# Delta-rule stage: calls of TensorE, ScalarE and VectorE in another order, the first heads' solve steps between the levels of the second half's inverse

## The chip, the core and the metric

The kernel runs on one core of a Trainium2 chip. The metric is device time in microseconds for one launch, and less is better. A core has TensorE (PE, matrix products, with its weight loads shown apart as PEld), VectorE (DVE), ScalarE (ACT, functions looked up in a table set that is loaded beforehand), GpSimd (POOL) and DMA queues, here all issued by SyncE (SP). The engines run side by side, each through its own list of instructions in the order in which the program was written, and they wait for each other on semaphores.

## The reference, cut to what matters

Two blocks of two layers each for 256 tokens of width 1024 in fp32. The change touches only the gated delta rule of the second block:

```python
def gdn_mixer(h, w_in, conv_w, a_log, dt_bias, o_norm, w_out):
    proj = h @ w_in
    qkv, z, a, b = jnp.split(proj, [3 * W, 4 * W, 4 * W + H], axis=-1)
    qkv = jax.nn.silu(causal_depthwise_conv(qkv, conv_w))
    q, k, v = jnp.split(qkv, 3, axis=-1)
    q, k = l2_norm(q), l2_norm(k)               # per head of 128
    beta = jax.nn.sigmoid(b)
    g = -jnp.exp(a_log) * jax.nn.softplus(a + dt_bias)
    o = chunk_gated_delta_rule(q, k, v, g, beta)
    o = rms_norm_2(o, o_norm) * jax.nn.silu(z)
    return o @ w_out
...
def chunk_gated_delta_rule(q, k, v, g, beta):
    gcum = jnp.cumsum(gc, axis=-1)
    decay = jnp.where(causal, jnp.exp(gcum[..., :, None] - gcum[..., None, :]), 0.0)
    a_mat = jnp.where(strict, jnp.einsum('bhncd,bhnsd->bhncs', kb, kc) * decay, 0.0)
    sol = lax.linalg.triangular_solve(a_mat, rhs, left_side=True, lower=True, unit_diagonal=True)
    u, w = sol[..., :Dv], sol[..., Dv:]
    attn = jnp.einsum('bhncd,bhnsd->bhncs', qc, kc) * decay
    ...
```

There are 8 heads of 128. Before and after this stage, the change leaves every call where it was.

## The kernel before, in words

**Weights.** All weights are cut into 136 chunks of at most 128 x 2048. A chunk is loaded by DMA into one of three `raw` buffers, ACT copies it to a rounded half (`hi(c)`, `whi<-raw`), DVE subtracts to get the rest (`lo(c)`, `wlo<-raw,whi`), and PE multiplies both halves in four quarters, `quarter(c, 0..3)`. On PE a call `to(c, q)` issues every quarter up to `(c, q)`. The delta-rule stage has chunks 94 to 114: 94 to 106 make k, q and v, 107 to 110 make z, 111 to 114 are the output product. A chunk's `hi` waits until PE has done all four quarters of the chunk three before it.

**The delta rule in 128-token tiles.** For head h, `conv_pre(i)` (DVE), `conv_acc(i)` (ACT) and `conv_taps(i)` (DVE, six instructions) are the convolution of two of the 24 column groups, `conv_silu` and `v_silu` its silu. `qk_square(h)` (ACT), `sums(h)` (PE) and `sum_add(h)` (DVE) are the norms; `ln_sums` (ACT) takes the logarithm of all of them. `row_bc(h)` (PE, `ps<-spread,pick`) spreads a row of log decays over the partitions, `decay_arg(h)` (DVE) adds the column part, `decay(h)` (ACT, two instructions) exponentiates, `kq(h)` (PE, `ps<-arena`) makes the products of keys with keys and queries, and `block_(h)` (DVE) multiplies them by the decays.

**The inverse and the solve.** Heads go in groups g of two (0 to 3; heads 0 to 3 are the first half, 4 to 7 the second). The triangular inverse of a group starts from 8x8 blocks (`inv_c`, `inv_d`, `inv_r`, `inv_b`, `inv_e`, `inv_0`) and doubles them in the levels 3 to 6: `inv_w`, `inv_x` and `inv_v` on PE, with a copy out of PSUM on ACT (`inv_w`, `inv_y`) and an addition on DVE (`inv_x`) between them; `inv_f`, `inv_t`, `inv_y` finish it. The solve of head h has four steps on PE, `sol(h, 0)` to `sol(h, 3)`, with ACT copying out of PSUM after the steps 0, 2 and 3 and DVE after step 1. Then the output norm: `out_squares`, `rsq("gdn_o0")` (ACT: a logarithm, then an exponential), `rsq_b`, `out_norm`, `out_T`, `out_hi`, `out_lo`.

**What sets the order.** It is written out by hand, one list of calls for each engine (PE from L1223, ACT from L2190, DVE from L3500, POOL from L3815), and an engine never runs a call ahead of one that stands before it. Small products of PE share four PSUM banks, 4 to 7, taken in turn (`ring`, L505): a call that takes a bank first waits until the engine that reads the call four banks back has read it. So `row_bc` and `kq` also wait for the decays (semaphore `g_ed`, one count for each `decay(h)`) and for the blocks (`g_ba`) of earlier heads, and `sol(3, 3)` waits for ACT's copy of `sol(3, 2)` (`g_sa3`).

**Tables.** `table(name)` (L1469) asks for a table set by an explicit load. Where an activation's function isn't in the set that is loaded at that place of ACT's list, the build puts a load of its own ahead of that activation; it then bears the line of the activation (L1467 before, L1469 after) and not that of `table`. In the kernel before, every function finds its set loaded by `table`.

Of the kernel before, what the change touches and what calls it, by code (L numbers as in the profile page):

```python
# [131 lines left out]
def bass_two_blocks(nc, A, out):  # L132

    ctx = ExitStack()
    with ctx:
# [358 lines left out]
        def tensor_program(eng):  # L494
# [745 lines left out]
            to(104, 2)  # L1240
            sums(6)
            sums(7)
            to(105, 0)
            rw_T()
            kq(0)
            row_bc(0)
            row_bc(1)
            to(106, 0)
# [12 lines left out]
            kq(5)  # L1261
            inv_c(0)
            row_bc(6)
            to(108, 0)
            inv_r(0)
            row_bc(7)
            to(108, 1)
            kq(6)
            to(109, 0)
            inv_0(1)  # L1270
            inv_0(0)
            kq(7)
            to(109, 1)
            inv_w(1, 3)
            inv_w(0, 3)
            to(109, 2)
            inv_x(0, 3)
            inv_x(1, 3)
            to(109, 3)
            inv_v(0, 3)  # L1280
            inv_v(1, 3)
            inv_w(0, 4)
            inv_w(1, 4)
            v_T(0, 0)
            v_T(0, 1)
            inv_x(0, 4)
            inv_x(1, 4)
            to(110, 0)
            v_T(1, 0)
            inv_v(1, 4)  # L1290
            inv_w(1, 5)
            v_T(1, 1)
            inv_v(0, 4)
            inv_w(0, 5)
            inv_x(1, 5)
            to(110, 1)
            inv_x(0, 5)
# [15 lines left out]
            sol(0, 0)  # L1313
            sol(1, 0)
            to(111, 0)
            inv_y(1)
# [13 lines left out]
            sol(2, 1)  # L1330
            inv_x(2, 3)
            inv_v(3, 3)
            inv_w(3, 4)
            inv_v(2, 3)
            sol(3, 1)
# [128 lines left out]
        def scalar_program(eng):  # L1464
# [4 lines left out]
            def table(name):  # L1469
                eng.preload_act_table_set(name)  # L1470
# [755 lines left out]
            qk_square(1)
            conv_silu(4)
            hi(105)
            conv_silu(5)
            conv_acc(7)  # L2230
            qk_square(2)
            qk_square(3)
            conv_silu(6)
            qk_square(4)
            qk_square(5)
            conv_silu(7)
# [15 lines left out]
            decay(5)  # L2252
            decay(6)
            hi(110)
# [1908 lines left out]
```

How the kernel before makes its waits and increments, by code:

```python
    def wait_ge(self, sem, v):  # L58
        if self.seen.get(sem.num, 0) < v:
            self.seen[sem.num] = v
            self.e.wait_ge(sem, v)
# [6 lines left out]
    def settle(self, n=None):  # L68
        self.wait_ge(self.own, self.n if n is None else n)
# [429 lines left out]
            def take(b, sem_, v):  # L499
                if hold[b] is not None:
                    L.wait_ge(*hold[b])
                hold[b] = (sem_, v)
# [20 lines left out]
            def x_ready(stage, j2):  # L524
                L.wait_ge(s_xlo, 4 * XROUND[stage] + j2 + 1)
# [1 line left out]
            def x_ready_kv(j2, t):  # L527
                L.wait_ge(s_flo, 4 * t + j2 + 1)
# [1 line left out]
            def quarter(c, q):  # L530
                d = CHUNKS[c]
                kind, stage = d["kind"], d["st"]
                wh, wl = wk(whi, c), wk(wlo, c)
                if c < 2 and q == 0:
                    if c == 1:
                        L.wait_ge(s_l0, 4)
                elif c == SPLIT:
                    if q == 0:
                        L.wait_ge(s_l0, 8)
                    elif q == 1:
                        L.wait_ge(*LO[c])
                elif 2 <= c < 5 and q % 2 == 0:
                    L.wait_ge(*((s_l0, c + 3) if q == 0 else LO[c]))
                elif q == (1 if kind == "uq" else 0):
                    if stage[:3] == "mlp" and kind == "pw" and (c not in UP or d["hk"] == 0):
                        L.wait_ge(s_hi, c + 1)
                    else:
                        L.wait_ge(*LO[c])
                tok = None
# [3343 lines left out]
            def finish():  # L3893
                eng.wait_ge(s_out, 80)
```

## Time and profile before

| | |
|---|---|
| median of 3 runs | 893.73 us (893.17 to 894.28) |
| the profiled execution, its own time | 893.27 us |
| its span | 891.1 us |
| PE / PEld busy | 881.4 / 767.6 us (99 / 86%) |
| DVE / ACT / POOL busy | 632.1 / 521.7 / 38.6 us (71 / 59 / 4%) |
| mean granted clock of TensorE | 1.000 |
| HBM | 141.85 MB read, 160 GB/s over the span |
| table loads on ACT | 8, of 1283 ns each, 3 of them in the delta-rule stage |

A busy share is the time in which an engine has an instruction running. Matmuls are pipelined: each shows a duration longer than the distance to the next one, so starts are compared with starts. The span lies from the first to the last instruction; the rest of the 893.27 us lies around it. Times in rows are microseconds from the start of the span. Where the same kind of instruction stands several times in a row, the trace's order merges them into one line with a count.

### The profile page before, as it was taken

What the parts mean: (1) busy time and instruction counts of PE and PEld (TensorE: products, weight loads), DVE (VectorE), ACT (ScalarE), POOL (GpSimd) and SP (SyncE); (2) the same over time, 40 slices, a digit from 0 to 9 for tenths busy, and PEclk for the clock granted to TensorE, in tenths of its full rate; (3) what the DMA queues carried; (4) which work ended last, traced back from release to release, by engine and by line L of the source; (5) the groups of instructions that cost most, each with busy time, mean ns of one, the idle gap of its engine ahead of it and who ended that gap; (6) DMA issues with size and microseconds to landing.
All of it is one profiled execution on the core that took longest, in us unless ns stands there. A gap on an engine that the chain in (4) does not pass through costs nothing.

```text
span 891.1 us, 13047 instructions
## 1 busy us (share of the span) xinstructions
PE 881.4 (99%) x5231; PEld 767.6 (86%) x5231; DVE 632.1 (71%) x1067; ACT 521.7 (59%) x851; POOL 38.6 (4%) x48
## 2 busy tenths in 40 slices
PE   9999999999999999999999999999999999999997
PEld 8878888888888888888888888999989987798885
DVE  7986877766575667567656556679899867767774
ACT  6997443454445677645444435466556756747782
POOL 0151000000000000000000000000014310000000
PEclk9999999999999999999999999999999999999999
DMA  8722455454745454347455654555241312654511
GB/s 313 242 95 100 185 167 211 163 193 166 248 149 188 143 189 158 126 150 242 176 194 183 223 197 150 157 177 182 65 180 49 121 46 66 219 213 142 189 48 47
DMA packets 60876, 143.72 MB, mean 161 GB/s; under 512 B 4497, under 2 KB 6673, under 8 KB 60817
## 3 DMA queue, kind: packets, MB, share of 16 engines
q1 hardware_dynamic: 60816, 142.91, 46.3%
q8 instruction: 41, 0.67, 0.3%
q14 instruction: 19, 0.15, 0.0%
HBM read 141.85 MB, written 1.05 MB: 160 GB/s over the span
## 4 chain that ended last, share of the span: by engine, by line
PE 95%; DVE 2%; ACT 2%; DMA 1%; issue 0%; SPq 0%; DVEq 0%
PE ps L513 90%; PE ps L521 5%; ACT arena L1467 1%; DMA raw<-mla_w_in_dram 1%; ACT whi L1467 0%; DVE arena_r L2456 0%; DVE sub L2456 0%; DVE arena L2766 0%; DVE wlo L2456 0%; ACT xhl L1467 0%; DVE X L2462 0%; DVE st L2462 0%; ACT L1470 0%; DVE arena L2456 0%; DVE xhl L2462 0%
## 5 line engine op out<-in xcount | busy, mean ns | idle before, releaser
L2456 DVE TENSOR_TENSOR wlo<-raw,whi 128x2048 fp32r<-128x2048 f32 (+4 forms) x141 | 300.0, 2137 | 104.8 <-ACT whi L1467 104.7
L1467 ACT ACTIVATE whi<-raw 128x2048 fp32r<-128x2048 f32 (+6 forms) x143 | 251.6, 1771 | 158.5 <-PE ps L513 144.0
L513 PE MATMUL ps<-xhl,whi 128*128 128x512 f32 (+1 forms) x912 | 199.6, 346 | 0.0
L513 PEld LDWEIGHTS ps<-xhl,whi 128*128 128x128 f32 x912 | 155.1, 188 | 19.9 <-DVE xhl L2462 0.2
L513 PE MATMUL ps<-whi,xhl 128*128 128x512 f32 (+2 forms) x528 | 167.2, 385 | 0.4 <-DVE xhl L2462 0.3
L513 PE MATMUL ps<-whi,oth 128*128 128x512 f32 x416 | 165.4, 398 | 0.0
L513 PE MATMUL ps<-whi,otl 128*128 128x512 f32 x416 | 162.3, 390 | 0.0
L513 PE MATMUL ps<-wlo,oth 128*128 128x512 f32 x416 | 162.1, 390 | 0.0
L513 PE MATMUL ps<-xhl,wlo 128*128 128x256 f32 x704 | 121.6, 283 | 0.0
L513 PEld LDWEIGHTS ps<-whi,xhl 128*128 128x128 f32 x528 | 98.3, 189 | 18.4 <-issue 1.8
L513 PEld LDWEIGHTS ps<-xhl,wlo 128*128 128x128 f32 x704 | 103.0, 191 | 3.2 <-DVE wlo L2456 0.2
L513 PE MATMUL ps<-wlo,xhl 128*128 128x512 f32 (+2 forms) x264 | 99.3, 378 | 0.3 <-DVE wlo L2456 0.3
L513 PEld LDWEIGHTS ps<-whi,otl 128*128 128x128 f32 x416 | 78.1, 188 | 16.7
L513 PEld LDWEIGHTS ps<-whi,oth 128*128 128x128 f32 x416 | 78.2, 188 | 15.5 <-issue 0.3
L513 PEld LDWEIGHTS ps<-wlo,oth 128*128 128x128 f32 x416 | 78.2, 188 | 15.0
L1467 ACT ACTIVATE arena<-ps 128x256 f32<-128x256 f32 (+4 forms) x138 | 52.2, 417 | 66.3 <-PE ps L513 61.2
L2456 DVE TENSOR_TENSOR arena<-ps,arena 128x256 f32<-128x256 f32 (+3 forms) x106 | 46.7, 469 | 40.6 <-ACT arena L1467 28.2
L513 PE MATMUL ps<-arena 128*128 128x128 f32 (+3 forms) x384 | 64.0, 318 | 0.5 <-ACT arena L1467 0.5
L513 PEld LDWEIGHTS ps<-arena 128*128 128x128 f32 (+1 forms) x384 | 54.6, 190 | 7.0 <-issue 1.6
L1467 ACT ACTIVATE arena<-ps,st 128x512 f32<-128x512 f32 (+2 forms) x64 | 39.4, 643 | 33.1 <-PE ps L513 15.1
L513 PEld LDWEIGHTS ps<-wlo,xhl 128*128 128x128 f32 x264 | 49.6, 188 | 7.7 <-DVE wlo L2456 0.6
L1467 ACT ACTIVATE arena<-arena 128x512 f32<-128x512 f32 (+4 forms) x68 | 39.4, 606 | 4.1 <-DVE arena L2462 2.2
(150 smaller groups left out, 827.3 us busy)
## 6 DMA issues: line engine op xcount, KB each, us to landing
raw<-mlp_w_in_dram SPq DMA_DIRECT2D x32, 1024.0 KB, 5.3
raw<-mlp_w_out_dram SPq DMA_DIRECT2D x32, 1024.0 KB, 4.9
raw<-gdn_w_in_dram SPq DMA_DIRECT2D x16, 1024.0 KB, 5.3
raw<-moba_w_qkv_dram SPq DMA_DIRECT2D x12, 1024.0 KB, 5.1
raw<-kv_w_dram SPq DMA_DIRECT2D x8, 1024.0 KB, 5.4
raw<-fox_w_in_dram SPq DMA_DIRECT2D x8, 1024.0 KB, 5.1
raw<-mla_w_o_dram SPq DMA_DIRECT2D x4, 1024.0 KB, 4.8
raw<-moba_w_o_dram SPq DMA_DIRECT2D x4, 1024.0 KB, 6.2
```

Source lines behind the costliest of these rows:

```text
L513: return eng.matmul(o, l, r, start=start, stop=True, skip_group_check=True)
L521: return eng.transpose(o, i, ident)
L1467: return eng.activation(o, i, f, **kw)
L2456: return eng.tensor_tensor(o, a, b, f)
```

## The change

Nothing is added to or taken from the program as it is written, except that `table("natural_log_exp_and_others")` ahead of `ln_sums()` is gone, that `table("silu_and_others")` and `table("natural_log_exp_and_others")` now stand together behind `decay(1)`, where one `table("silu_and_others")` stood behind `decay(7)`, and that calls stand in another order. On PE the small products and the quarters of weights they stand between are in another order from chunk 101 to chunk 112. `decay(h)` calls on ACT now have `conv_acc`, `v_silu(0)` and `hi` between them in another pattern. The diff, cut to the places that matter:

```diff
 # PE
+            kq(1)
+            row_bc(2)
+            to(105, 3)
+            row_bc(3)
             to(106, 1)
-            row_bc(3)
             kq(2)
-            to(106, 3)
+            to(106, 2)
+            kq(3)
             row_bc(4)
+            row_bc(5)
+            to(107, 0)
+            kq(4)
+            row_bc(6)
             to(107, 1)
-            kq(3)
-            kq(4)
-            row_bc(5)
+            kq(5)
+            row_bc(7)
+            to(107, 2)
+            inv_c(0)
             to(107, 3)
-            kq(5)
-            inv_c(0)
-            row_bc(6)
...
             inv_0(3)
+            sol(2, 0)
             inv_0(2)
             sol(0, 2)
-            sol(2, 0)
+            sol(1, 2)
             inv_w(3, 3)
+            sol(3, 0)
             inv_w(2, 3)
-            sol(3, 0)
-            sol(1, 2)
...
-            sol(2, 2)
+            inv_x(3, 4)
             sol(3, 2)
-            inv_x(3, 4)
+            sol(2, 1)
             inv_x(2, 4)
             sol(3, 3)
+            sol(2, 2)
             inv_v(3, 4)
             inv_v(2, 4)
+            inv_w(2, 5)
+            out_T(0)
+            inv_w(3, 5)
+            inv_x(2, 5)
             sol(2, 3)
 # ACT
             qk_square(7)
-            table("natural_log_exp_and_others")
             ln_sums()
-            conv_acc(8)
-            conv_acc(9)
+            hi(107)
             decay(0)
             decay(1)
-            hi(107)
+            table("silu_and_others")
+            table("natural_log_exp_and_others")
+            conv_acc(8)
             decay(2)
+            decay(3)
+            conv_acc(9)
+            conv_acc(10)
             hi(108)
-            decay(3)
             decay(4)
-            hi(109)
+            v_silu(0)
             decay(5)
             decay(6)
-            hi(110)
             decay(7)
-            table("silu_and_others")
-            conv_acc(10)
+            hi(109)
+            z_silu(0, 0)
+            inv_0(1)
             conv_acc(11)
-            v_silu(0)
-            inv_0(1)
...
             inv_w(2, 4)
-            sol(2, 2)
+            rsq("gdn_o0")
             sol(3, 2)
             table("natural_log_exp_and_others")
-            rsq("gdn_o0")
             sol(3, 3)
+            sol(2, 2)
 # DVE
             decay_arg(0)
             decay_arg(1)
-            conv_taps(8)
+            conv_pre(9)
             block_(0)
             lo(107)
             block_(1)
-            conv_taps(9)
-            inv_0(0)
             decay_arg(2)
             decay_arg(3)
+            conv_taps(8)
+            conv_taps(9)
             block_(2)
+            conv_pre(10)
+            inv_0(0)
             decay_arg(4)
-            conv_pre(10)
+            block_(3)
+            decay_arg(5)
```

**ACT, the decays of heads 4 to 6, before.** `arena<-ps5,st 128x256` and its like are the first instruction of a `decay`, `arena<-arena 128x2x256` the second; `whi1<-raw1` is `hi(109)`, `whi2<-raw2` is `hi(110)`.

```order
L1467 ACTIVATE arena<-ps5,st 128x256 [waits g_dt]
L1467 ACTIVATE arena<-arena 128x2x256
L1467 ACTIVATE whi1<-raw1 128x2048 [waits s_w,s_raw1]
L1467 ACTIVATE arena<-ps6,st 128x256 [waits g_dt]
L1467 ACTIVATE arena<-arena 128x2x256
L1467 ACTIVATE arena<-ps6,st 128x256 [waits g_dt]
L1467 ACTIVATE arena<-arena 128x2x256
L1467 ACTIVATE whi2<-raw2 128x2048 [waits s_w,s_raw2]
L1467 ACTIVATE arena<-ps4,st 128x256 [waits g_dt]
L1467 ACTIVATE arena<-arena 128x2x256
```

And now; `arena<-arena 128x1024` is `v_silu(0)`, `arena<-arena,small` is `conv_acc(10)`:

```order
L1469 ACTIVATE arena<-arena,small 128x256 [waits g_pre]
L1469 ACTIVATE arena<-arena,small 128x256
L1469 ACTIVATE whi0<-raw0 128x2048 [waits s_w,s_raw0]
L1469 ACTIVATE arena<-ps7,st 128x256 [waits g_dt]
L1469 ACTIVATE arena<-arena 128x2x256
L1469 ACT_TABLE_LOAD
L1469 ACTIVATE arena<-arena 128x1024 [waits g_cv]
L1469 ACT_TABLE_LOAD
L1469 ACTIVATE arena<-ps4,st 128x256 [waits g_dt]
L1469 ACTIVATE arena<-arena 128x2x256
```

`v_silu(0)` stands between `decay(4)` and `decay(5)`, with a load that the build placed on each side of it, and `conv_acc(10)` and `hi(108)` stand ahead of `decay(4)`; `hi(109)` moved behind `decay(7)`.

**PE, the keys' products of head 5, before.** `ps0` and `ps1` with `whi2,xhl` are quarters of chunk 107, `arena 128x2x128` opens `kq(5)` (four instructions), `own8,otl` is `inv_c(0)`, `spread,pick` is `row_bc(6)`.

```order
L513 MATMUL ps1<-whi2,xhl 128x512 [waits g_pre]
L513 MATMUL ps1<-wlo2,xhl 128x512
L513 MATMUL ps1<-whi2,xhl 128x512 x2
L513 MATMUL ps1<-wlo2,xhl 128x512
L513 MATMUL ps1<-whi2,xhl 128x512
L513 MATMUL ps7<-arena 128x2x128 [waits g_ba]
L513 MATMUL ps4<-arena 128x128
L513 MATMUL ps7<-arena 128x2x128
L513 MATMUL ps4<-arena 128x128
L513 MATMUL ps5<-own8,otl 128x8 [waits g_id1,g_id0]
L513 MATMUL ps5<-own8,otl 128x8 x7
L513 MATMUL ps6<-spread,pick 128x2x128 [waits g_ed]
```

And now, where the first `spread,pick` is `row_bc(6)`, then comes one quarter of chunk 107, `kq(5)`, and `row_bc(7)`:

```order
L513 MATMUL ps7<-spread,pick 128x2x128 [waits g_ed]
L513 MATMUL ps7<-spread,pick 128x2x128
L513 MATMUL ps0<-whi2,xhl 128x512 [waits g_pre,s_lod]
L513 MATMUL ps0<-wlo2,xhl 128x512
L513 MATMUL ps0<-whi2,xhl 128x512 x2
L513 MATMUL ps0<-wlo2,xhl 128x512
L513 MATMUL ps0<-whi2,xhl 128x512
L513 MATMUL ps4<-arena 128x2x128 [waits g_ba,g_ed]
L513 MATMUL ps5<-arena 128x128
L513 MATMUL ps4<-arena 128x2x128
L513 MATMUL ps5<-arena 128x128
L513 MATMUL ps6<-spread,pick 128x2x128 x2
```

Two quarters of chunk 107 that stood ahead of `kq(5)` now stand behind it, `row_bc(6)` now stands ahead of it, and it now waits for `g_ed`, which for this bank is the count of `decay(5)`, beside `g_ba`.

**ACT, the first output norm, before.** The first row is the copy of `inv_w(2, 4)`, the two `st<-st` are `rsq("gdn_o0")`, `arena<-ps` with `g_sp2`, `g_sp3` the copies of `sol(2, ..)` and `sol(3, ..)`, those of 128x256 of their last steps.

```order
L1467 ACTIVATE arena_r<-ps6 128x512 [waits g_ip2]
L1467 ACTIVATE arena<-ps7 128x128 [waits g_sp2]
L1467 ACTIVATE arena<-ps4 128x128 [waits g_sp3]
L1470 ACT_TABLE_LOAD
L1467 ACTIVATE st<-st 128x4 [waits s_rm]
L1467 ACTIVATE st<-st 128x4 [waits o_act]
L1467 ACTIVATE arena<-ps7 128x256 [waits g_sp3]
L1467 ACTIVATE arena_r<-ps4 128x512 [waits g_ip3]
```

And now, from the copies of `inv_y(2, 3)` and `inv_w(2, 4)` on:

```order
L1469 ACTIVATE arena_r<-ps4 128x512 [waits g_ip2]
L1469 ACTIVATE arena_r<-ps5 128x512 [waits g_ip2]
L1469 ACT_TABLE_LOAD
L1469 ACTIVATE st<-st 128x4 [waits s_rm]
L1469 ACT_TABLE_LOAD
L1469 ACTIVATE st<-st 128x4 [waits o_act]
L1469 ACTIVATE arena<-ps7 128x128 [waits g_sp3]
L1472 ACT_TABLE_LOAD
L1469 ACTIVATE arena<-ps6 128x256 [waits g_sp3]
L1469 ACTIVATE arena<-ps7 128x128 [waits g_sp2]
```

`rsq("gdn_o0")` stands ahead of the copy of `sol(3, 2)`, with a load ahead of each of its two instructions, and the load of `table` follows behind that copy.


Beside these, the build places loads of its own ahead of `ln_sums()`, `decay(0)` and `z_silu(0, 0)`. With them and those of the rows above ACT's list has 15 loads in place of 8: 10 from `ln_sums()` to `rsq("gdn_o0")` in place of 3.

## Rows read from the trace of the kernel before

**Rows 1.** The page: chain that ended last, shares of the span by engine
```profile
PE 95%; DVE 2%; ACT 2%; DMA 1%; issue 0%; SPq 0%; DVEq 0%
```

**Rows 2.** Windows: span, busy us (count) of PE, PEld, DVE, ACT, POOL; clock; DMA
```profile
630.00:697.00 67.00, 67.00 (x464) 61.83 (x463) 61.14 (x123) 36.93 (x56) 14.08 (x10) 1.00 0.26 94
697.00:718.00 21.00, 20.26 (x161) 18.78 (x160) 15.94 (x41) 17.55 (x39) 7.32 (x7) 1.00 0.48 176
```

**Rows 3.** Waits of PE: who waited for whom, us in total, times, longest us
```profile
PE ps L521 <- DVE arena_r L2456: 0.6, 2, 0.3
...
PE ps L521 <- DVE X L2462: 0.3, 1, 0.3
```

**Rows 4.** Timeline of ACT: start us, us, instruction, xcount, [idle before <-releaser]
```profile
629.54 1.28 ACT L1470 ACT_TABLE_LOAD   x1
...
665.65 0.63 ACT L1467 ACTIVATE arena<-arena 128x512 f32<-128x512 f32 x1
666.30 1.28 ACT L1470 ACT_TABLE_LOAD   x1
667.59 1.71 ACT L1467 ACTIVATE arena<-arena,small 128x256 f32<-128x256 f32 x4
```

**Rows 5.** Timeline of PE around the end of quarter (104, 3)
```profile
634.54 0.38 PE L521 MATMUL ps<-small,st 128*32 128x128 f32 x2
```

**Rows 6.** Timeline of ACT: the two instructions of decay(4), then hi(109)
```profile
652.19 0.48 ACT L1467 ACTIVATE arena<-ps,st 128x256 f32<-128x256 f32 x1
652.55 0.64 ACT L1467 ACTIVATE arena<-arena 128x512 f32<-128x512 f32 x1
653.07 1.92 ACT L1467 ACTIVATE whi<-raw 128x2048 fp32r<-128x2048 f32 x1
```

**Rows 7.** Groups of ACT, 597 to 730 us, shapes apart: v_silu
```profile
L1467 ACT ACTIVATE arena<-arena 128x1024 f32<-128x1024 f32 x2 | 2.1, 1063 | 0.0
```

**Rows 8.** Timeline of DVE: decay_arg(0) and (1), conv_taps(8), block_(0), lo(107)
```profile
636.51 1.66 DVE L2462 SCALAR_TENSOR_TENSOR arena<-ps,st,cap 128x256 f32<-128x256 f32 x4 [0.54 <-PE ps L513]
638.09 2.45 DVE L2462 SCALAR_TENSOR_TENSOR arena<-arena,small 128x255 f32<-128x255 f32 x6
640.45 1.02 DVE L2462 SCALAR_TENSOR_TENSOR arena<-ps,arena 128x512 f32<-128x512 f32 x2
641.38 2.28 DVE L2456 TENSOR_TENSOR wlo<-raw,whi 128x2048 fp32r<-128x2048 f32 x1
```

**Rows 9.** Timeline of PE: kq(1), row_bc(4), last product of quarter (107, 2), kq(5)
```profile
642.30 1.47 PE L513 MATMUL ps<-arena 128*128 128x256 f32 x8
...
649.70 0.47 PE L513 MATMUL ps<-spread,pick 128*128 128x256 f32 x2
...
658.40 0.39 PE L513 MATMUL ps<-whi,xhl 128*128 128x512 f32 x1
658.63 1.47 PE L513 MATMUL ps<-arena 128*128 128x256 f32 x8
```

**Rows 10.** Timeline of ACT: from the copy of inv_y(3, 3) to rsq("gdn_o0")
```profile
707.07 2.20 ACT L1467 ACTIVATE arena_r<-ps 128x512 fp32r<-128x512 f32 x4
709.17 0.44 ACT L1467 ACTIVATE arena<-ps 128x128 f32<-128x128 f32 x2
709.63 1.28 ACT L1470 ACT_TABLE_LOAD   x1
710.92 0.45 ACT L1467 ACTIVATE st<-st 128x4 f32<-128x4 f32 x2
```

**Rows 11.** Timeline of PE: inv_0(3) and (2), sol(3, 3), inv_v(2, 5)
```profile
701.00 1.32 PE L521 MATMUL ps<-small,arena_r 128*128 128x128 f32 x8 [0.29 <-DVE arena_r L2456]
...
709.94 0.88 PE L513 MATMUL ps<-arena 128*128 128x128 f32 x6
...
715.03 0.66 PE L521 MATMUL ps<-small,arena_r 128*128 128x128 f32 x4 [0.32 <-DVE arena_r L2456]
```

**Rows 12.** Timeline of PE: the first matmuls of the program
```profile
1.18 4.85 PE L513 MATMUL ps<-spread 128*128 128x256 f32 x21 [1.18 <-DVE spread L2758]
```

More of the change, by code:

```diff
@@ L1312, in tensor_program @@
             to(110, 3)
-            sol(0, 0)
             sol(1, 0)
             to(111, 0)
+            sol(0, 0)
             inv_y(1)
@@ L2263, in scalar_program @@
             inv_w(1, 3)
-            inv_y(0, 3)
+            hi(110)
             inv_y(1, 3)
-            inv_w(0, 4)
             inv_w(1, 4)
             v_silu(1)
+            inv_y(0, 3)
+            inv_w(0, 4)
             hi(111)
@@ L2276, in scalar_program @@
             inv_w(1, 6)
+            z_silu(0, 1)
             inv_y(0, 5)
@@ L2279, in scalar_program @@
             inv_t(0)
-            z_silu(0, 0)
-            z_silu(0, 1)
+            z_silu(1, 0)
+            sol(1, 0)
             inv_t(1)
-            z_silu(1, 0)
             sol(0, 0)
-            sol(1, 0)
             hi(113)
             inv_0(3)
+            sol(2, 0)
             inv_0(2)
             sol(0, 2)
-            sol(2, 0)
+            sol(1, 2)
+            sol(3, 0)
             inv_w(3, 3)
             inv_w(2, 3)
-            sol(3, 0)
-            sol(1, 2)
             z_silu(1, 1)
@@ L3545, in vector_program @@
             rT_copy()
-            conv_pre(9)
+            conv_pre(8)
             decay_arg(0)
             decay_arg(1)
-            conv_taps(8)
+            conv_pre(9)
             block_(0)
@@ L3552, in vector_program @@
             block_(1)
-            conv_taps(9)
-            inv_0(0)
             decay_arg(2)
             decay_arg(3)
+            conv_taps(8)
+            conv_taps(9)
             block_(2)
+            conv_pre(10)
+            inv_0(0)
             decay_arg(4)
-            conv_pre(10)
-            lo(108)
-            block_(3)
-            block_(4)
-            inv_0(1)
-            decay_arg(5)
-            lo(109)
+            block_(3)
+            decay_arg(5)
+            inv_0(1)
+            conv_pre(11)
+            block_(4)
+            decay_arg(6)
+            lo(108)
             block_(5)
             inv_d(0)
-            decay_arg(6)
             decay_arg(7)
+            inv_0(2)
             inv_b(0)
-            conv_pre(11)
             inv_e(1)
@@ L3577, in vector_program @@
             block_(7)
-            inv_0(3)
+            inv_x(1, 3)
             inv_x(0, 3)
-            inv_x(1, 3)
+            v_beta(0, 0)
             lo(110)
-            v_beta(0, 0)
+            inv_x(1, 4)
             v_beta(0, 1)
-            inv_0(2)
-            inv_x(1, 4)
             inv_x(0, 4)
             v_beta(1, 0)
+            inv_0(3)
             lo(111)
-            v_beta(1, 1)
             inv_x(1, 5)
             inv_x(0, 5)
+            v_beta(1, 1)
             lo(112)
@@ L3601, in vector_program @@
             inv_b(1)
-            inv_e(2)
             inv_e(3)
@@ L3605, in vector_program @@
             sol(1)
+            inv_e(2)
             sol(0)
@@ L3608, in vector_program @@
             inv_x(3, 3)
+            inv_x(2, 3)
+            out_sums(0)
+            sol(3)
+            inv_x(3, 4)
             sol(2)
-            inv_x(2, 3)
-            sol(3)
-            out_sums(0)
-            inv_x(3, 4)
+            rsq_b("gdn_o0")
             inv_x(2, 4)
-            rsq_b("gdn_o0")
             out_norm(0)
+            out_lo(0)
             inv_x(2, 5)
-            out_lo(0)
             inv_x(3, 5)
@@ L3625, in vector_program @@
             inv_s(2)
+            inv_f(2)
             inv_s(3)
-            inv_f(2)
             inv_f(3)
             inv_y(2)
+            out_lo(1)
             inv_y(3)
-            out_lo(1)
+            sol(4)
             sol(5)
-            sol(4)
             sol(7)
```

137 lines of the change are left out of this document (65 added, 72 removed).

## The prediction, made before the changed kernel ran

> **What bounds the kernel now.** I read the chain first: PE holds 95% of it [rows 1]. Then the windows of the delta-rule stage: PE is busy for all of 630 to 697 and for 20.26 of the next 21 us [rows 2]. Then PE's waits: in the whole stage the views show three over 0.25 us, two for DVE's inverse and one of 0.3 for the residual behind the output product [rows 3, 11]. So PE has hardly anything to gain: its instructions are the same before and after, and what an order can bring is the sum of these waits and some tenths that pass when PE changes from one kind of product to another, about 1.8 us. What an order can cost has no such bound, since each small product waits on DVE or ACT, and ACT is busy for 17.55 of the 21 us of the second half [rows 2]. So I looked last at the timeline of ACT and at what its list now holds.
>
> **What is added on ACT.** The written calls are the same but for one `table`, yet the list now has 10 table loads from `ln_sums()` to `rsq("gdn_o0")` in place of 3, since `table` no longer stands where the function's kind changes and the build fills in. A load shows 1.28 us; the one at 666.30 begins 0.02 us after the second instruction of a decay ends (665.65 + 0.63) and the next activation starts 0.01 us behind it [rows 4]. So I price a load at 1.28 us of ACT, and seven more at 9.0 us. ACT is busy for 36.93 of 67 us in the first part, so most of it could lie in idle time; what counts is which loads stand ahead of something that PE waits for.
>
> The page "ScalarE: Activation LUTs" of the Trainium skill (What ACT_TABLE_LOAD costs) gives the same 1283 ns and adds a drain of some 1380 ns for every switch to another set, 2.66 us in all. The rows show no such gap on either side of a load [rows 4], so the sum goes without it; with it, it would be the rival named below.
>
> **First half, in the time base of before.** Four steps.
>
> 1. `hi(107)` now stands ahead of `decay(0)`. It needs all quarters of chunk 104, whose last ends at 634.7 (the next product starts at 634.54 and the tail of the pipeline is 0.16) [rows 5]. It takes 1.9 [rows 6], so it ends at 636.6. The build's load follows to 637.9, `decay(0)` to 638.9 and `decay(1)` to 639.8 (0.99 for one, 0.90 more for the next) [rows 6]. PE is at `kq(1)` 2.9 us earlier than at 642.30, since two quarters of 12 products at 0.12 moved behind it: 639.4 [rows 9]. By the banks it needs `decay(1)`. Wait: 0.45.
> 2. The two loads of `table` stand behind `decay(1)`: ACT is at `conv_acc(8)` at 642.4 and done at 643.3. DVE does `block_(0)` from 638.95, `lo(107)`, `block_(1)` and two `decay_arg`, 0.93 + 2.2 + 0.93 + 1.6, to 644.6, so that the two loads are hidden. Then it does `conv_taps(8)` and `(9)`, 2.37 each, to 649.35 and `block_(2)` to 650.4 [rows 8]. PE's `row_bc(4)` needs that block's bank. It comes to it at 649.70 + 1.23 for `kq(3)`, now ahead, less 1.44 for a quarter, now behind, plus the 0.45 of step 1: 649.95 [rows 9]. Wait: 0.45.
> 3. `conv_acc(10)` on ACT waits for `conv_pre(10)`, 0.6 us behind `block_(2)` on DVE; it runs from 651.0 to 651.85, `hi(108)` to 653.65, `decay(4)` to 654.6 [rows 6]. Then a load, `v_silu(0)` with 1.06 [rows 7], a load: 658.25. `decay(5)` ends at 659.25.
> 4. PE's `kq(5)` needs `decay(5)` by its bank. It stood at 658.63; two quarters of six products at 0.23 moved behind it and `row_bc(6)` with 0.32 ahead of it: 656.2, and with the waits so far 657.1 [rows 9]. It starts at 659.3. Wait: 2.2.
>
> Together 3.1. A wait of PE is not made good later in this stage, since PE has no idle time there [rows 2]. Behind `kq(5)` stand the quarters of chunks 107 and 108 and all of the first inverse; DVE's `block_(5)` and `inv_d(0)` wait for PE in turn, and so ACT's `decay(7)`, `hi(109)` and DVE's `lo(109)` come late by about the same, not by more: I find `lo(109)` done at 672.9 and PE at quarter (109, 0) at 675.7. The load ahead of `z_silu(0, 0)` falls where ACT waits for PE anyway, and costs nothing; if it weren't covered it would cost 1.28. That the order of the first half itself saves nothing I take from the calls issued up to quarter (110, 1), which are the same. I book 3.2, for the first matmul behind a wait starts with its weights not yet loaded (some 0.05 each). The bounds: without any cost of the build's loads, `decay(0)` to `decay(5)` come 1.3 to 3.9 us earlier and no step waits, so 0; with every load that stands ahead of `decay(5)` on the path (1 + 2 + 2) and nothing hidden, 6.4.
>
> **Second half, in the time base of before.** PE's `inv_0(2)` now waits for DVE's `inv_e(2)`, which moved behind `inv_y(1)` and `sol(1)`: about 0.5, in place of the 0.29 at 701.00 [rows 11]. That is even. Then `rsq("gdn_o0")` moved ahead of the copy of `sol(3, 2)`. Of the four copies at 707.07 the last ends at 709.27 [rows 10]; the order brings it to 709.1. A load to 710.4, the logarithm 0.24, a load to 711.9, the exponential 0.2, and the copy of `sol(3, 2)` 0.28: 712.4 [rows 10]. PE's `sol(3, 3)` needs that copy; it stood at 709.94 [rows 11], and comes to 709.7 with `sol(2, 2)` behind it. It starts at 712.45, 2.5 us later than before. Behind it stand ten small products and their copies. The load of `table` puts ACT at the copies of `sol(3, 3)` and of `inv_y(3, 4)` at 713.7, so `inv_x(2, 5)`, `inv_x(3, 5)` and `inv_v(2, 5)` wait 0.3, 0.3 and 0.15 by my count, in place of the 0.32 and 0.25 that PE waits there before (at 715.03 and behind it) [rows 11]. Even again. So 2.5. Bounds: 0, if the two loads lay in idle time, and 3.9, if the third load is paid too.
>
> **What is moved and costs nothing.** On PE 1.3 to 1.8 us of waits could go in the second half; the two entries above keep them. Behind chunk 111 the solve of the last four heads has the same distance from copy to use (four steps of 0.22). `hi(114)` and `lo(114)` moved ahead of `out_hi(2)` and `out_lo(2)`; these end at 737.8 where PE comes to quarter (113, 0) at about 737.9, so this is covered only just, and would cost a tenth or two. The wait of 0.3 for the residual [rows 3] is there before and after, since it hangs on the last product of the stage. The DMA queue's list is the same, and a load of weights starts when DVE is done with the chunk three before it; DMA is busy for 0.26 of the time [rows 2].
>
> **Sum.** 893.27 for the profiled execution, of which 891.1 is the span, and 3.2 + 2.5: 899.0. The execution lies 0.46 under the median of the runs shown, 893.73, so by the median it would be 899.4; I say 899.1. A difference under 0.2% (1.8 us) I count as no change.
>
> **Rivals.**
>
> - *The loads are free.* If ACT loads a set that it has at hand in no time, or if all seven fall into idle time, the order's own saving stays: in the second half PE comes to inv_v(3, 5) 1.8 us earlier, less 0.5 for `inv_0(2)`. That gives 892.0, faster. For it speaks that ACT is idle for 30 of the 67 us [rows 2]; against it that the load in rows 4 takes its full time with work right behind it, and that it decides only if `decay(5)` is done by 657.1, two loads earlier than counted. 5%.
> - *Part is hidden.* One of the two waits of 2 us is shorter, because DVE's blocks come earlier than I count or because ACT reaches a load early: 896.0 to 897.5. The first wait hangs on a chain of fifteen durations. 12%, and 3% more that both are mostly hidden: 893 to 895.
> - *More waits behind the long ones.* The copies of the second half are tight on every engine (waits under 0.1 us everywhere by my reading), and each load that I hid could show: one more load, 1.28, and a few tenths: 900.5 to 902.5. 12%.
> - *The clock falls.* All rows show a granted clock of 1.00 (2.4 GHz). PE idles 2.2 and 2.7 us at once, where before it never idled over 0.5 in this stage. The first 21 products of the program, behind an idle engine, stand 0.23 apart [rows 12], the same shape later 0.12. If PE ran at 1.2 GHz for two quarters behind each wait, that would add 2 x 2.8: 904.6. Nothing in the rows shows a fall inside the program. 5%.
> - *A drain with each load.* 1.38 more for each of the three loads on the path to `decay(5)` and the two ahead of `sol(3, 2)`: 6.9 more, 906. 2%, for the rows speak against it.
>
> **Numbers.** Forecast 899.1 with 61%, 898.0 to 900.5. The range: below, it takes in the part-hidden case, above, that of more waits: 896.3 to 903.0. Faster 5% (free loads), same 3% (both waits mostly hidden), slower 92%.
>
> **What would show it.** In the profile after: ACT_TABLE_LOAD 15 times; a wait of PE of some 2 us for ACT's `arena` in the product `ps<-arena 128x256` around 657 to 659, two of 0.4 to 0.5 in the 18 us before it; one of 2.5 to 2.8 us around 713 to 716 in `ps<-arena 128x128`, with two loads, an `st<-st` between them, running on ACT meanwhile; PE's clock at 1.00. Wrong would be: no wait over 1 us, or a time under 896, or waits of PE for `wlo`, which I expect nowhere.

## The result, and the profile after

The changed kernel takes 904.0 us (median of four executions, 901.26 to 905.98) against 893.75 for the kernel before, timed beside it: a ratio of 1.0113, 95% interval 1.0085 to 1.014. That is slower, as forecast, but by 10.3 us where 5.7 were booked, and above the range. The profiled execution took 903.99 us, 10.72 more than the one of before; its span is 901.8.

The page of the changed kernel: busy time by engine, and the shares of the chain that ended last (which answer to [rows 1]).

```profile
PE 886.1 (98%) x5231; PEld 771.4 (86%) x5231; DVE 633.4 (70%) x1067; ACT 530.6 (59%) x858; POOL 41.8 (5%) x48
...
PE 91%; ACT 4%; DVE 3%; DMA 1%; issue 0%; POOL 0%; SPq 0%; DVEq 0%; ACTq 0%
```

PE's share of the chain fell by 4 points, ACT's rose by 2 and DVE's by 1. PE's waits (engine, waited for, us in total, times, longest), against [rows 3]; the one for `wlo` lies at 7.13 us, at the start of the program, where the kernel before waits 0.33:

```profile
PE ps L513 <- ACT arena L1469: 6.1, 4, 2.5
...
PE ps L513 <- DVE wlo L2458: 0.6, 1, 0.6
PE ps L513 <- POOL otl L3776: 0.3, 1, 0.3
PE ps L521 <- DVE arena_r L2458: 0.3, 1, 0.3
```

Waits alone explain little more than half of the 10.7 us. Windows of the same trace, over the whole of the two halves and then in steps of 4 us around three places (columns as in [rows 2], the granted clock behind POOL's):

```profile
630.00:704.00 74.00, 70.47 (x462) 64.17 (x463) 62.05 (x123) 43.28 (x60) 16.56 (x10) 0.95 0.25 86
704.00:728.00 24.00, 21.08 (x157) 19.93 (x155) 15.36 (x39) 19.35 (x38) 8.00 (x7) 0.93 0.41 154
```

```profile
626.00:630.00 4.00, 4.00 (x38) 4.00 (x36) 3.41 (x3) 3.22 (x3) 0.00 (x0) 1.00 0.81 260
630.00:634.00 4.00, 4.00 (x22) 4.00 (x23) 2.09 (x13) 0.84 (x2) 0.00 (x0) 0.57 0.72 265
657.00:661.00 4.00, 1.96 (x11) 1.37 (x9) 3.89 (x6) 3.96 (x5) 0.00 (x0) 1.00 0.02 4
661.00:665.00 4.00, 3.67 (x13) 3.23 (x14) 1.30 (x3) 1.16 (x3) 0.00 (x0) 0.58 0.57 182
665.00:669.00 4.00, 4.00 (x23) 3.43 (x22) 2.42 (x5) 0.59 (x2) 2.12 (x2) 1.00 0.20 80
715.00:719.00 4.00, 1.99 (x18) 1.84 (x16) 1.29 (x5) 3.95 (x6) 2.27 (x2) 1.00 1.04 416
719.00:723.00 4.00, 3.48 (x19) 3.48 (x20) 2.14 (x8) 2.91 (x8) 0.00 (x0) 0.57 0.92 342
723.00:727.00 4.00, 3.93 (x34) 3.68 (x33) 2.10 (x4) 3.37 (x8) 2.28 (x2) 1.00 0.02 4
```

In three windows the granted clock is 0.57 or 0.58 on the mean: of the two levels, 1.2 GHz for 3.4 of the 4 us. Where it is low, PE gets through fewer matmuls while it shows as busy: 22 from 630 to 634, where the kernel before has 37. The kernel before shows 1.00 in all of the stage [rows 2]. (At the very end of the program, where PE has nothing left to do, every profiled execution shows half clock for 0.7 to 3.9 us, that of before too. It costs no matmul, but takes up to 0.002 off the mean clock of an execution.) Timeline of PE at these three places (start, us, instruction, count, idle before and releaser):

```profile
627.70 2.78 PE L513 MATMUL ps<-cst,arena 128*128 128x1 f32 x24
630.33 0.78 PE L513 MATMUL ps<-xhl,whi 128*128 128x256 f32 x2
...
633.68 0.40 PE L513 MATMUL ps<-xhl,whi 128*128 128x256 f32 x2
...
641.91 1.55 PE L513 MATMUL ps<-arena 128*128 128x256 f32 x8 [0.70 <-ACT arena L1469]
...
661.33 2.93 PE L513 MATMUL ps<-arena 128*128 128x256 f32 x8 [2.36 <-ACT arena L1469]
...
719.52 2.08 PE L513 MATMUL ps<-arena 128*128 128x128 f32 x8 [2.54 <-ACT arena L1469]
```

The first row is `sums(5)`, `(6)` and `(7)`, 24 products of one column each, now in a row, since quarter (104, 1) moved behind them. The pair of 128x256 takes 0.78 right behind them and 0.40 at 633.68. The other two stretches lie at the two long waits: the eight matmuls of `kq(5)`, 1.47 before [rows 9], take 2.93 at 661.33.

ACT ahead of `kq(5)` (up to the first instruction of `decay(5)` at 660.28) and ahead of `sol(3, 3)`, against [rows 4, 6, 7] and [rows 10]:

```profile
638.59 1.28 ACT L1469 ACT_TABLE_LOAD   x1
...
641.78 2.57 ACT L1472 ACT_TABLE_LOAD   x2
...
656.61 1.28 ACT L1469 ACT_TABLE_LOAD   x1
657.91 1.06 ACT L1469 ACTIVATE arena<-arena 128x1024 f32<-128x1024 f32 x1
658.99 1.28 ACT L1469 ACT_TABLE_LOAD   x1
660.28 0.47 ACT L1469 ACTIVATE arena<-ps,st 128x256 f32<-128x256 f32 x1
...
716.29 1.28 ACT L1469 ACT_TABLE_LOAD   x1
717.58 0.21 ACT L1469 ACTIVATE st<-st 128x4 f32<-128x4 f32 x1
717.81 1.28 ACT L1469 ACT_TABLE_LOAD   x1
719.10 0.21 ACT L1469 ACTIVATE st<-st 128x4 f32<-128x4 f32 x1
719.21 0.26 ACT L1469 ACTIVATE arena<-ps 128x128 f32<-128x128 f32 x1
719.49 1.28 ACT L1472 ACT_TABLE_LOAD   x1
```

The loads stand where the list put them, and PE waits for what is behind them. So the theory to test: ACT's loads make two long waits, and these and the streak of one-column products each let TensorE's clock fall for a while.

The count in the two profiled executions goes by one stretch that both have: from the last small product ahead of the delta-rule stage (`ps<-pick,arena`) to the first residual product behind it (`ps<-small,X`), before and then now:

```profile
584.38:748.37 163.99, 162.92 (x1183) 152.16 (x1183) 136.45 (x277) 98.87 (x166) 21.40 (x16) 1.00 0.33 113
584.52:759.08 174.56, 168.01 (x1183) 156.24 (x1183) 137.59 (x277) 107.77 (x173) 24.56 (x16) 0.97 0.31 106
```

The same 1183 matmuls take 10.6 us more. PE is idle for 6.55 us of it in place of 1.07, 5.5 more: waits of 0.70, 0.15 (`row_bc(4)`), 2.36, 0.32 (`inv_w(1, 5)`, for POOL), 0.31 (`inv_0(2)`) and 2.54 us, 6.38 together, less the 0.94 of before that went (0.29, 0.32 and the 0.33 for the residual [rows 3, 11]). And PE is busy for 5.1 us more with the same matmuls. That goes with the three stretches at half clock: 3.4 us of it can cost 1.7 at most, and about 1.5 each is an estimate, since PE idles for the first 0.3 to 0.5 us of two of them. Some tenths of the 5.1 are then not the clock's.

The executions differ in how often the clock falls, and the longer ones mostly have the lower mean clock: the four of the changed kernel have a mean clock of 0.993, 0.993, 0.992 and 0.998 at 903.99, 904.02, 905.98 and 901.26 us.

### The profile page after: what moved, and what is told of

It reads as the page before. It is cut to its first block, busy times and chain, and to the rows that moved or that the text cites. A ratio compares the mean times of both kernels' runs of the same rounds, so it can differ in the third digit from the quotient of the medians.

```text
span 901.8 us, 13053 instructions
## 1 busy us (share of the span) xinstructions
PE 886.1 (98%) x5231; PEld 771.4 (86%) x5231; DVE 633.4 (70%) x1067; ACT 530.6 (59%) x858; POOL 41.8 (5%) x48
## 4 chain that ended last, share of the span: by engine, by line
PE 91%; ACT 4%; DVE 3%; DMA 1%; issue 0%; POOL 0%; SPq 0%; DVEq 0%; ACTq 0%
PE ps L513 86%; PE ps L521 4%; ACT arena L1469 1%; DVE arena L2464 1%; ACT whi L1469 1%; ACT L1469 1%; DMA raw<-mla_w_ukv_dram 1%; DMA raw<-mla_w_in_dram 1%; DVE wlo L2458 1%; POOL otl L3776 0%; DVE arena L2458 0%; DVE sub L2458 0%; DVE arena_r L2458 0%; ACT arena_r L1469 0%; DVE X L2464 0%
## 5 line engine op out<-in xcount | busy, mean ns | idle before, releaser
L513 PE MATMUL ps<-arena 128*128 128x128 f32 (+3 forms) x384 | 67.2, 327 | 6.1 <-ACT arena L1469 6.1
L513 PEld LDWEIGHTS ps<-arena 128*128 128x128 f32 (+1 forms) x384 | 56.5, 196 | 13.5 <-ACT arena L1469 7.1
L3776 POOL TENSOR_TENSOR otl<-arena,level_mask 128x512 fp32r<-128x512 f32 x8 | 14.8, 1866 | 610.8 <-PE ps L513 610.8
```

Source lines behind the costliest of these rows:

```text
L513: return eng.matmul(o, l, r, start=start, stop=True, skip_group_check=True)
L3776: return eng.tensor_tensor(o, a, b, f)
```

## The experiments

Each is a median over four to eleven executions, beside 20 or so of the kernel before (893.67 to 894.06); ratios are to those, with 95% intervals. For the profiled executions, the table behind the experiments splits the same stretch as above into idle and busy time of PE.

**Only the first half's loads put right.**

```diff
+            table("natural_log_exp_and_others")
             ln_sums()
 ...
             decay(1)
-            table("silu_and_others")
-            table("natural_log_exp_and_others")
 ...
             decay(4)
-            v_silu(0)
             decay(5)
             decay(6)
             decay(7)
+            table("silu_and_others")
+            v_silu(0)
```

> The changed kernel with ACT's tables of the first half put right: one load ahead of ln_sums, the pair behind decay(1) gone, v_silu(0) moved behind decay(7) with a load ahead of it; ACT's list has 10 loads. Loads theory (ACT's extra loads make the long waits, and a long wait makes PE run at 1.2 GHz for a while): the wait of 2.36 us of kq(5) and the half-clock stretch behind it go, the wait of 2.54 us of sol(3,3) and its half-clock stretch stay, as does the one behind the three sums in a row: 904.0 - 2.4 - 0.9 - 1.4 to 1.9, so 898.8 to 899.3. Rival, the order of the calls on PE and DVE makes the waits and the loads lie in idle time: kq(5) still waits over 1.5 us, 903 to 904. Rival, the clock falls by the order alone: the wait goes but the clock still falls near 660 us, 900.5 to 901.

Measured: 898.26 us, ratio 1.0049 [1.0034, 1.0064], 5.7 under the changed kernel. In the first half no wait over 0.2 us is left up to `inv_w(1, 5)`; `sol(3, 3)` still waits 2.54, and behind it the clock falls. It went a little further than expected. The rivals that the order makes the wait of `kq(5)`, or brings the clock down near 660 us by itself, are out. The edit also takes `v_silu(0)` (1.06 us) from ahead of `decay(5)`; that loads alone are enough is shown by the six loads further down. The six executions run from 895.61 (mean clock 0.999) to 900.20 (0.992): by these mean clocks the wait of 2.54 doesn't always bring the fall.

**Only the second half's loads put right.**

```diff
             inv_w(2, 4)
-            rsq("gdn_o0")
             sol(3, 2)
             table("natural_log_exp_and_others")
+            rsq("gdn_o0")
             sol(3, 3)
```

> The changed kernel with rsq(gdn_o0) behind the copy of sol(3,2) on ACT, and its table ahead of it; 13 loads. Loads theory: the wait of 2.54 us of sol(3,3) goes and with it the half-clock stretch at 719 us, the first half stays: 904.0 - 2.5 - 1.4 to 1.9, so 899.6 to 900.1. Rival, the order makes the wait: sol(3,3) still waits over 1.5 us, 903 to 904. Rival, the clock falls by the order alone: wait gone, clock still low near 717 us, 901.5.

Measured: 900.1 us, 1.0068 [1.0056, 1.008]. The wait of `sol(3, 3)` is gone and the time is as the loads theory gave it. But a wait of 1.15 us appeared at `inv_v(2, 4)`, three calls later, which the expectation had not counted, and the profiled execution has one half-clock stretch (behind `kq(5)`, which waits 2.35) and none at 630 us, where two were expected. So the agreement in time is partly luck.

**Both.** The two diffs above together.

> Both corrections: ACT's list has 8 loads, as before the change, all other calls in the new order. Loads theory: no wait of PE over 1 us, one half-clock stretch left (behind the three sums in a row, at 630 us): 892.5 to 895. Rival, the order costs what the loads were charged with: over 899. Rival, the half-clock stretch at 630 us is an effect of what follows: clock at 1.00 everywhere, 892 to 893.

Measured: 896.14 us (11 executions), 1.0021 [1.0013, 1.003]: over the expected 892.5 to 895, so the order costs something by itself. The profiled execution (895.77) has no half-clock stretch in the stage. It is 1.0 us longer there than before, with the wait of 1.15 at `inv_v(2, 4)`; another 1.5 us had come up ahead of the stage, where nothing was changed. The rest of the median's 2.4 this trace doesn't show.

**Both, and a quarter between the sums again.** On PE; `to(104, 2)` stops ahead of quarter (104, 2), so the quarter that it puts here is (104, 1):

```diff
             sums(5)
+            to(104, 2)
             sums(6)
             sums(7)
```

> Both corrections, and on PE quarter (104,1) again between sums(5) and sums(6), sums(7), as before the change. Loads theory with the clock falling behind a streak of products that leave PE little to do: clock at 1.00 everywhere, 1.4 to 1.9 us under the kernel with both corrections, 891 to 893.3. Rival, the streak has no part in the clock's fall at 630 us: same time as with both corrections, within 0.4 us, and the clock is low there or in both of them nowhere.

Measured: 895.37 us (11), 1.0016 [1.0007, 1.0024]: 0.8 under the one without, between the two theories. The two intervals overlap, so this run doesn't decide on the quarter; the next one does. It is still 1.6 over before. What remains in the trace, in PE's timeline of this kernel:

```profile
712.92 0.66 PE L521 MATMUL ps<-small,arena_r 128*128 128x128 f32 x4 [1.15 <-DVE arena_r L2459]
713.33 0.64 PE L513 MATMUL ps<-arena_r 128*128 128x128 f32 x4
713.96 0.66 PE L521 MATMUL ps<-small,arena 128*128 128x128 f32 x4
```

The first is `inv_v(2, 4)`. It needs DVE's `inv_x(2, 4)`, which the change put behind `rsq_b("gdn_o0")`, and that waits for ACT's `rsq`. In the changed kernel this wait was hidden: PE sat at `sol(3, 3)` meanwhile. The last row is `out_T(0)`.

**The sums' quarter moved in the kernel before.** One place on PE:

```diff
             to(104, 1)
             sums(5)
-            to(104, 2)
             sums(6)
             sums(7)
```

> The kernel before with one quarter, (104,1), moved from between sums(5) and sums(6), sums(7) to behind them, so that 24 products of one column stand in a row, as in the changed kernel; nothing waits. Theory that this streak lets TensorE's clock fall: a half-clock stretch near 630 us in some executions, and the median 0.5 to 1.6 us over before, 894.3 to 895.4. Rival, the fall at 630 us in the changed kernel came by chance or of something else: 893.5 to 894.0.

Measured: 895.58 us (11), 1.0017 [1.0008, 1.0026], 1.9 slower. The window from 631 to 636 us in its trace, and the same of the kernel before:

```profile
631.00:636.00 5.00, 5.00 (x32) 5.00 (x31) 2.38 (x13) 1.03 (x3) 0.00 (x0) 0.66 0.46 173
```

```profile
631.00:636.00 5.00, 5.00 (x42) 4.88 (x41) 3.20 (x15) 1.03 (x3) 0.00 (x0) 1.00 0.42 163
```

PE is busy for all 5 us in both, and makes 32 matmuls in place of 42. The only wait is one of 0.17 us for ACT inside the streak, and the changed kernel had none there. So the clock falls behind a streak of small products that the profile counts as busy, with next to no idle time.

**The same place in the changed kernel,** whose loads all stay:

```diff
             sums(5)
+            to(104, 2)
             sums(6)
             sums(7)
```

> The changed kernel with quarter (104,1) again between sums(5) and sums(6), sums(7), all loads as they are. Theory that the three sums in a row drop the clock by themselves (the same one-place change cost the kernel before 1.9 us): 904.0 - 1.9, 901.7 to 902.5. Rival, with the long waits behind it the fall at 630 us makes no difference: 903.5 to 904.2.

Measured: 902.16 us (4), 1.0089 [1.0075, 1.0103], 1.8 under the changed kernel, as the theory has it. But the interval overlaps with the changed kernel's (1.0085 to 1.014), so this difference by itself isn't clear of noise. In its profiled execution the stretch at 630 us is gone, and the wait of 2.35 us at `kq(5)` brings no fall, the one of 2.54 us does.

**Loads where nothing waits.** In the kernel before, four loads in ACT's idle 7.5 us:

```diff
             hi(107)
+            table("silu_and_others")
+            table("natural_log_exp_and_others")
+            table("silu_and_others")
+            table("natural_log_exp_and_others")
             decay(2)
```

> The kernel before with four more table loads on ACT (5.1 us of ACT) in its idle time of 7.5 us behind hi(107), ahead of decay(2). Theory that a load costs only where it stands ahead of something that PE waits for: no change, 893.4 to 894.1. Rival, loads cost wherever they stand (a drain, or disturbed DMA): 0.5 us or more each, over 895.5.

Measured: 893.63 us (11), 1.0001 [0.9992, 1.001]. Covered loads are free, within 0.9 us for four.

**Loads ahead of `decay(5)`.** In the kernel before, six between `hi(109)` and `decay(5)`:

```diff
             hi(109)
+            table("silu_and_others")
+            table("natural_log_exp_and_others")
+            table("silu_and_others")
+            table("natural_log_exp_and_others")
+            table("silu_and_others")
+            table("natural_log_exp_and_others")
             decay(5)
```

> The kernel before with six more table loads on ACT (7.7 us) between hi(109) and decay(5), all other calls as before: decay(5) ends at about 663.7 and the product that needs it stood at 660.75, so PE waits about 2.95 us once. Theory wait and clock: the wait and a half-clock stretch right behind it in most executions, 893.75 + 2.95 + 1.0 to 1.7, so 897.7 to 898.4. Rival, the clock's falls in the changed kernel come of its order and not of a wait: 893.75 + 2.95, so 896.5 to 897.0, clock at 1.00 throughout the stage.

Measured: 899.54 us (5), 1.0064 [1.0051, 1.0076]: 5.9 slower, over both theories. ACT and PE in its timeline, and its windows:

```profile
655.47 7.72 ACT L1470 ACT_TABLE_LOAD   x6
...
664.25 0.80 PE L513 MATMUL ps<-spread,pick 128*128 128x256 f32 x2 [2.94 <-ACT arena L1467]
```

```profile
661.00:665.00 4.00, 1.06 (x6) 0.97 (x6) 0.69 (x2) 3.18 (x4) 2.21 (x2) 0.81 0.79 256
665.00:669.00 4.00, 4.00 (x12) 3.23 (x11) 2.21 (x6) 2.26 (x3) 0.00 (x0) 0.50 0.02 6
669.00:673.00 4.00, 4.00 (x18) 3.33 (x18) 3.59 (x16) 3.81 (x7) 0.00 (x0) 0.84 0.00 0
```

The wait is the 2.94 that the sum gave. By these three means (0.19, 0.50 and 0.16 of 4 us short of full speed, twice that in time at the lower level) the clock is low for 6.8 us, twice as long as in the changed kernel, and costs the other 2.9 us. The order is that of before, so the new order isn't needed for the fall.

**Fewer loads at that place.** The edit lists five names with two equal ones in a row; the build makes one load of these, so four run:

```diff
             hi(109)
+            table("silu_and_others")
+            table("natural_log_exp_and_others")
+            table("silu_and_others")
+            table("silu_and_others")
+            table("natural_log_exp_and_others")
             decay(5)
```

> The kernel before with five more table loads (6.4 us) between hi(109) and decay(5) in place of six: by the trace with six, where PE waited 2.94 us, PE waits 1.65 us here. With six the time rose by 5.9 us, 2.9 of it the half-clock stretch of 6.83 us. Theory wait and clock: the longer the wait, the more often and the longer the clock falls behind it; here it falls in some executions: 893.7 + 1.65 + 0.5 to 1.7, 895.9 to 897.1. Rival, each extra load costs 1 us of its own (5.9 for six): 898.6. Rival, a wait of this length does nothing to the clock: 895.2 to 895.5.

Measured: 894.09 us (11), 1.0003 [0.9994, 1.0012]. The expectation counted a load too many:

```profile
655.13 5.15 ACT L1470 ACT_TABLE_LOAD   x4
...
661.34 0.50 PE L513 MATMUL ps<-spread,pick 128*128 128x256 f32 x2 [0.35 <-ACT arena L1467]
```

Four loads leave a wait of 0.35 us and cost next to nothing; two more, 2.6 us of ACT, cost 5.5. The mean clock of the eleven executions is 0.996 to 0.999, as in the kernel before, that of the five with six loads 0.995 or 0.996. That is the most direct measure of the second half of the theory. A wait between the two sizes was not tried.

**PE given work in place of the wait.** The changed kernel with all its loads, two quarters ahead of `kq(5)`:

```diff
             row_bc(6)
-            to(107, 1)
+            to(107, 3)
             kq(5)
             row_bc(7)
-            to(107, 2)
             inv_c(0)
-            to(107, 3)
             inv_r(0)
```

> The changed kernel with all of its 15 loads, and on PE the quarters (107,1) and (107,2) ahead of kq(5) as before the change, so that PE has 2.9 us of work where it waited 2.36 us for decay(5); row_bc(7) goes with kq(5). Theory that the idle time makes the clock fall: no wait over 1 us and no half-clock stretch near 660 us, 904.0 - 2.36 - 1.35, so 900.0 to 900.8. Rival, the load alone is what counts and the products behind come late by as much: 903 to 904.

Measured: 902.35 us (4, 899.88 to 903.96), 1.0096 [1.008, 1.0111]: 1.7 under the changed kernel, half of what was expected, and with overlapping intervals. The profiled execution is the shortest of the four (899.88, mean clock 0.997; the others 0.993 to 0.995), so it doesn't show where the others lost time. In it `kq(5)` waits no more and no clock falls there; part of the wait reappears at `inv_r(0)`, whose operand from DVE comes later:

```profile
660.16 1.47 PE L513 MATMUL ps<-arena 128*128 128x256 f32 x8
...
663.51 0.50 PE L513 MATMUL ps<-otl,blk 128*128 128x512 f32 x1 [0.85 <-DVE otl L2456]
```

**The wait of `inv_v(2, 4)` removed.** Added to the kernel with both corrections and the quarter, on DVE:

```diff
             sol(2)
-            rsq_b("gdn_o0")
             inv_x(2, 4)
+            rsq_b("gdn_o0")
```

> The kernel with both corrections on ACT and the quarter between the sums, and in addition on DVE inv_x(2,4) ahead of rsq_b(gdn_o0) instead of behind it. In the trace without this, inv_v(2,4) on PE waits 1.14 us for inv_x(2,4), which on DVE stands behind rsq_b, which waits for ACT's rsq. Theory that this wait is the order's own cost: the wait goes and the time falls by 0.9 to 1.2, to 894.1 to 894.5, level with before within 0.1%. Rival, the rest over before (1.6 us) is spread over the order or lies elsewhere: 895.0 to 895.5.

Measured: 897.62 us (5, 895.96 to 898.56), 1.004 [1.0027, 1.0054]: 2.2 slower, where 1.1 faster was expected. The wait at `inv_v(2, 4)` is gone and PE stands at `out_T(0)` instead. DVE (a row of two of the four products of `out_norm(0)`), POOL and PE in its timeline:

```profile
713.19 1.53 DVE L2465 SCALAR_TENSOR_TENSOR arena<-arena,st 128x128 f32<-128x128 f32 x2
...
713.42 1.16 POOL L3777 TENSOR_TENSOR arena_r<-arena,level_mask 128x512 fp32r<-128x512 f32 x1 [1.55 <-PE ps L513]
...
715.04 0.65 PE L521 MATMUL ps<-small,arena 128*128 128x128 f32 x4 [1.70 <-DVE arena L2465]
```

And DVE and POOL of the kernel without this edit, all four products:

```profile
712.78 1.13 DVE L2465 SCALAR_TENSOR_TENSOR arena<-arena,st 128x128 f32<-128x128 f32 x4
...
714.05 2.28 POOL L3777 TENSOR_TENSOR arena_r<-arena,level_mask 128x512 fp32r<-128x512 f32 x2 [2.82 <-PE ps L513]
```

Two products that take 0.6 together took 1.53, and POOL's mask product ran beside them; without the edit POOL starts when the four are done. So the end of `out_norm(0)` gained nothing from the earlier start, PE's wait of 1.15 became one of 1.70 at the next call, and the clock is low behind it, for 6.8 us over this window and the ones beside it:

```profile
716.00:720.00 4.00, 4.00 (x21) 4.00 (x20) 2.06 (x4) 2.01 (x4) 1.16 (x1) 0.50 0.19 71
```

That POOL holds DVE up is read from this one overlap; no run here varies it alone. The page "Perfetto Trace Analysis" of the Trainium skill (Optimizing Scalar/DVE Operations) says that the two engines share a read port of SBUF, and that a DVE operation that uses two ports holds it as an exclusive lock. That they share a port fits the overlap; that POOL held it, and that this DVE operation needs it, this run doesn't show.

**First half new, second half as before.** The kernel with both corrections and the quarter, and from quarter (110, 2) on the order of before on all engines:

```diff
             # PE, and ACT, DVE likewise from here
+            sol(0, 0)
             sol(1, 0)
             to(111, 0)
-            sol(0, 0)
 ...
```

> First half in the new order (table loads and the quarter between the sums put right), second half from quarter (110,2) on in the order of before, on every engine. It tells where the 1.6 us lie that remain with both corrections. Theory that they lie in the second half (waits of 1.14 us for inv_x(2,4)): 893.7 to 894.3. Rival, in the first half or spread: 895.0 to 895.5.

Measured: 894.03 us (11), 0.9998 [0.9989, 1.0007]. The new order of the first half costs nothing that is clear of noise; the 1.6 us that remained lie in the second half. The trace shows there the wait for `inv_x(2, 4)` behind `rsq_b`; that this is the whole of it is argued, since taking it away made another wait. No version here beats the kernel before.

**The same stretch in every profiled execution,** from `ps<-pick,arena` to the first `ps<-small,X`, less the 163.99 us of before (of which PE idles 1.07):

| | longer by, us | PE idle | PE busy | half-clock stretches |
|---|---|---|---|---|
| the changed kernel | 10.6 | 5.5 | 5.1 | 3 |
| first half's loads put right | 3.4 | 2.2 | 1.3 | 1 |
| second half's loads put right | 6.5 | 4.1 | 2.4 | 1 |
| both | 1.0 | 0.9 | 0.1 | 0 |
| both, and the quarter | 1.4 | 1.1 | 0.3 | 0 |
| both, the quarter, `inv_x` first | 4.5 | 1.5 | 3.0 | 1, of 6.8 us |
| before, sums in a row | 1.8 | 0.2 | 1.6 | 1 |
| before, four covered loads | -0.1 | 0.0 | -0.1 | 0 |
| before, six loads ahead of `decay(5)` | 5.9 | 2.9 | 2.9 | 1, of 6.8 us |
| before, four loads there | 0.6 | 0.4 | 0.2 | 0 |
| changed, two quarters ahead of `kq(5)` | 6.3 | 4.1 | 2.2 | 1 |
| changed, quarter between the sums | 7.9 | 5.6 | 2.3 | 1 |
| first half new, second as before | 0.3 | 0.2 | 0.1 | 0 |

The idle time adds up: the two corrections take away 3.3 and 1.4 us of it one by one, 4.6 together. The busy time follows the stretches: 0.3 or less more where there is none, 1.3 to 2.4 with one, 2.9 and 3.0 with one of 6.8 us, 5.1 with three.

## Why the prediction was right and wrong

The steps, by the prediction's own numbers.

- *Seven loads more, 1.28 us each, no drain.* Right: 15 loads, and the next activation starts 0.01 to 0.02 us behind each. The 906 us of the drain rival lie near the measured time by chance; the trace has no such gap.
- *`kq(1)` waits 0.45, `row_bc(4)` 0.45, `kq(5)` 2.2.* Measured 0.70, 0.15 and 2.36: 3.21 together against 3.1 added up (3.2 booked). The single waits are off by up to 0.3, and cancel. The chain over `hi(107)`, `decay`, `conv_acc(10)`, `hi(108)`, `v_silu(0)` and the loads on both sides was read rightly from the durations of before.
- *`inv_0(2)` waits 0.5 in place of 0.29.* 0.31. *`sol(3, 3)` comes 2.5 later.* It waits 2.54. *Waits of 0.3 behind it stay.* They went, and so did the 0.33 for the residual, which the prediction had before and after. *No wait for `wlo`.* Right for this stage. `inv_w(1, 5)` waits 0.32 for POOL, not counted.
- *Sum of the waits, 5.7.* Measured 5.5. With the waits alone the profiled execution would have taken about 898.9, so this part of the forecast was right.
- *PE's clock at 1.00.* **The step that failed.** The prediction wrote "PE idles 2.2 and 2.7 us at once, where before it never idled over 0.5", had the half speed of the first 21 products before it [rows 12], and still gave the fall 5% and left it out of the sum, because "nothing in the rows shows a fall inside the program". It couldn't: no row of before had such an idle time to show it behind. The evidence was missing, and was taken as evidence against. That rival's 904.6 us is within 0.6 of the measured time, but not by its own sum: 2 x 2.8 was too much for each and one too few, for there are three stretches, of about 1.5 each, and PE is busy for 5.1 us more in all. The third is behind `sums(5)` to `(7)`, an exchange of PE's calls that the prediction passed over since nothing waits there; alone it costs 1.9 us.

That the waits come from the loads is shown by undoing them in each half (-5.7 and -3.9 us) and by putting loads into the kernel before, covered (0) and uncovered (+5.9). That a long wait brings the clock down is shown by the four and six loads. Three things stay open. The medians of the parts don't add up: the two corrections and the quarter make 11.5 us one by one and 8.6 together. In the profiled executions the idle time does add up, so the difference lies with the clock and with the scatter of four to six executions (up to 4.7 us). How often a fall follows a given wait isn't measured. And the streak of sums showed no fall in the profiled executions of four of the six kernels that have it.

## What to carry to other kernels

Count a wait of TensorE twice: for its length, and for the stretch at half clock that may follow it. Here 2.4 us of idling cost about 4 where the clock fell, and 0.35 cost no more than itself. The same goes for a row of products with one column, which the profile shows as busy: keep wide products between them. And before taking a wait away, look which one stands next behind it on the same producer; here a wait of 1.15 us taken away became one of 1.70, with a fall of the clock.

## What was not expected of the hardware

- The granted clock fell from 2.4 to 1.2 GHz around the end of idle times of 2.94, 2.54, 2.36 and 1.70 us, and behind 24 products of 128x1 in 2.78 us with no idle time; each time for 3.4 us or twice that. A wait of 2.35 us at `kq(5)` brought a fall in one profiled execution (second half's loads put right) and none in another (changed, quarter between the sums). The page "TensorE: Matmul & The Clock Gate" of the Trainium skill (HAM oscillation) warns of idle gaps between matmuls that send the engine back to the low clock. It puts the danger at longer gaps than these; here the shorter ones were enough, and the measurement decides.
- A matmul of 128x256 pairs went from 0.40 to 0.63 us a pair at the low clock, and a pair and the `wlo` product behind it stood 0.64 from the next in place of 0.36; the 42 matmuls of 5 us became 32, with the low clock for part of them.
- A table load costs nothing where ACT is idle anyway (four of them: 0.0 us, interval -0.7 to +0.9).
